# Splitting the input of a gated feed-forward stage before its norm factor is known, and applying the factor where the products are read

## The reference, cut to what matters

```python
def rms_norm(x, g):                 # per token: x * rsqrt(mean(x*x) + eps) * g
def conv_glu_ffn(h, w_up, conv_w, w_down):      # first block, width 2816 twice
    up = causal_dwconv(h @ w_up, conv_w)        # 3 taps over tokens, per channel
    gate, val = jnp.split(up, 2, axis=-1)
    return (jax.nn.silu(gate) * val) @ w_down
def sq_relu_mlp(x, w_up, w_down):               # second model's blocks, width 4096
    h = jax.nn.relu(x @ w_up); return (h * h) @ w_down
# first block: x = x + mixer(norm(x)); x = x + conv_glu_ffn(norm(x)); x = norm(x)
# then twice:  h = h + concat(mixer, memory_attention)(norm(h)) @ w_out
#              h = h + sq_relu_mlp(norm(h))
```

## Time and profile before

| what | us |
|---|---|
| timed, median of 3 runs (lowest, highest) | 1092.79 (1085.38, 1100.64) |
| the profiled execution's own time | 1086.28 |
| its span, first to last instruction | 1084.5 |
| busy: PE, DVE, ACT, POOL | 1036.2, 681.2, 548.7, 91.5 |
| granted TensorE clock, mean | 0.993 |

### The profile page before, as it was taken

One profiled execution on the slowest core, in us unless ns is written; L12 is line 12 of the kernel. 1 busy time (PEld: TensorE's weight loads), 2 busy tenths in 40 slices (PEclk: granted clock), 3 DMA queues, 4 the chain that ended last, 5 costly groups with the idle time before them and its releaser, 6 DMA issues.

```text
span 1084.5 us, 20595 instructions
## 1 busy us (share of the span) xinstructions
PE 1036.2 (96%) x8615; PEld 993.9 (92%) x8615; DVE 681.2 (63%) x807; ACT 548.7 (51%) x714; POOL 91.5 (8%) x54
## 2 busy tenths in 40 slices
PE   4998999899999899999999999999999999999998
PEld 3988779899887799999989899999999989999998
DVE  4777365655375778778677575555566867655553
ACT  4554435443454565555556454444456765544442
POOL 0050021200010000000019510000000001000000
PEclk9999899999999999999999999999999999999999
DMA  6544232324261364554524355555554323655551
GB/s 251 195 157 155 78 117 85 111 79 156 78 221 74 121 231 160 204 216 163 180 87 144 129 190 194 199 182 205 182 176 147 118 79 120 219 205 178 209 178 55
DMA packets 24803, 168.77 MB, mean 156 GB/s; under 512 B 2753, under 2 KB 3137, under 8 KB 5154
## 3 DMA queue, kind: packets, MB, share of 16 engines
q1 hardware_dynamic: 23616, 164.64, 43.2%
q10 hardware_dynamic: 1122, 3.19, 0.9%
HBM read 166.76 MB, written 1.05 MB: 155 GB/s over the span
## 4 chain that ended last, share of the span: by engine, by line
PE 71%; DVE 14%; ACT 7%; POOL 4%; issue 3%; DMA 1%; SPq 0%; ACTq 0%; DVEq 0%
PE G L577 11%; PE G L578 11%; PE G L579 11%; PE D L577 8%; PE D L578 8%; PE D L579 8%; DVE wlo L1704 4%; ACT whi L1199 2%; PE M L578 2%; PE M L577 2%; PE M L579 2%; PE D L821 1%; POOL zp L551 1%; ACT ss L1655 1%; DVE cv L2072 1%
## 5 line engine op out<-in xcount | busy, mean ns | idle before, releaser
L1704 DVE TENSOR_TENSOR wlo<-raw,whi 128x2048 fp32r<-128x2048 f32 (+1 forms) x156 | 360.3, 2314 | 142.6 <-ACT whi L1199 142.5
L577 PE MATMUL G<-xh,whi 128*128 128x256 f32 (+1 forms) x1360 | 387.5, 285 | 12.2 <-DVE wlo L1704 6.6
L578 PE MATMUL G<-xl,whi 128*128 128x256 f32 (+1 forms) x1360 | 379.4, 279 | 0.0
L579 PE MATMUL G<-xh,wlo 128*128 128x256 f32 (+1 forms) x1360 | 379.2, 279 | 0.0
L1199 ACT ACTIVATE whi<-raw 128x2048 fp32r<-128x2048 f32 (+1 forms) x156 | 295.5, 1897 | 54.1 <-PE D L579 50.9
L577 PEld LDWEIGHTS G<-xh,whi 128*128 128x128 f32 (+1 forms) x1360 | 256.6, 189 | 21.8 <-DVE wlo L1704 9.7
L578 PEld LDWEIGHTS G<-xl,whi 128*128 128x128 f32 (+1 forms) x1360 | 256.7, 189 | 1.3 <-issue 1.2
L579 PEld LDWEIGHTS G<-xh,wlo 128*128 128x128 f32 (+1 forms) x1360 | 256.3, 188 | 0.0
L577 PE MATMUL D<-hh,whi 128*128 128x256 f32 x688 | 190.2, 276 | 3.0 <-DVE wlo L1704 1.9
L579 PE MATMUL D<-hh,wlo 128*128 128x256 f32 x688 | 190.0, 276 | 0.0
L578 PE MATMUL D<-hl,whi 128*128 128x256 f32 x688 | 190.0, 276 | 0.0
(11 more groups left out here) (377 smaller groups left out, 1350.3 us busy)
## 6 DMA issues: line engine op xcount, KB each, us to landing
raw<-wall_dram SPq DMA_DIRECT2D x152, 1024.0 KB, 4.8
raw<-wnarrow_dram SPq DMA_DIRECT2D x4, 768.0 KB, 4.4
x<-x_dram SPq DMA_DIRECT2D x4, 256.0 KB, 5.7
mem<-mem_dram ACTq DMA_DIRECT2D x1, 1024.0 KB, 5.2
out_dram<-x SPq DMA_DIRECT2D x4, 256.0 KB, 2.5
poolw<-pool_w_dram ACTq DMA_DIRECT2D x1, 576.0 KB, 7.0
cst<-cst_dram ACTq DMA_DIRECT2D x1, 416.0 KB, 8.9
lora<-lora_dram ACTq DMA_DIRECT2D x1, 256.0 KB, 6.7
```

The lines of the kernel that those rows point to most:

```text
L577: mm(out, w_h, hi, start=start, stop=False, skip_group_check=skip)
L578: mm(out, w_h, lo, start=False, stop=False, skip_group_check=skip)
L579: return mm(out, w_l, hi, start=False, stop=stop, skip_group_check=skip)
L1704: signal(tt(wlo[:, pan.slot, 0:w], raw[:, pan.slot, 0:w], f32(whi[:, pan.slot, 0:w]), SUB), "w_lo")
```

## The change

The gated stage now works as the squared-ReLU stages do. Each part of x is split into `mh`, `ml` (times the gain alone) as soon as its `wo` panel has been added; the squares are summed by POOL and then by four matmuls behind the first up panel; the factor is multiplied in by DVE when it reads an up panel's product into `upad`. ACT's copy from PSUM goes away, and its tap instructions now read `upad`. DVE's gating moves from right after the taps to behind the next panel split. The memory rows are scaled and split in the last groups of `ffn 0` (and for the second block, of `ffn 1`), now into `xh`, `xl`. All other norm inputs use `mh`, `ml`. Both strings of constant matmuls around `ffn 0` are gone.

```diff
-    W += [("mem_load",), ("panel", PAN["wo"]), ("panel", PAN["wo"] + 1), ("mem_squares",)]
-    W += [("panel", PAN["wo"] + 2), ("mem_stat",), ("panel", PAN["wo"] + 3)]
-    W += [("norm", 1), ("mem_scale", 0), ("mem_norm", 0), ("ffn", 0), ("squares", 2)]
+    W += [("mem_load",), ("panel", PAN["wo"]), ("part", 1, 0), ("panel", PAN["wo"] + 1), ("mem_squares",), ("part", 1, 1)]
+    W += [("panel", PAN["wo"] + 2), ("mem_stat",), ("part", 1, 2), ("panel", PAN["wo"] + 3), ("part", 1, 3)]
+    W += [("sums", 1), ("ffn", 0), ("squares", 2)]
...
+    LATE = [(NI1 - 4, NI1 - 3), (NI2 - 3, NI2 - 2)]
+    IN_B = ("in0q", "in0m", "in1", "in1b", "ffn", "ffn0", "ffn1")
```

On PE:

```diff
-            elif n == 1:
-                warm(19, "D0")
...
-                    if nu == 2 and js == 1 and u == 0:
-                        warm(11, "M1")
...
-                    if isinstance(j, int) and j == 0 and f:
-                        norm_stat(2 * f + 2)
+                    if isinstance(j, int) and j == 0 and u == 0:
+                        norm_stat(FNORM[f])
```

On ACT, in `up`:

```diff
-                        fn(upad[:, u, :, 2:T + 2], G[u][:, :, :], ACT.Copy)
+                        act.wait_ge(S(f"up_read{f}"), 2 * j + u + 1)
                         for s_ in range(2):
-                            ins = fn(cv[:, u, s_, :], G[u][:, s_, :], ACT.Copy, scale=w2)
-                        signal(ins, f"up_read{f}")
+                            signal(fn(cv[:, u, s_, :], upad[:, u, s_, 2:T + 2], ACT.Copy, scale=w2), "tap")
```

On DVE, in `up`, and what it calls:

```diff
+                        if u:
+                            gate(j, 0, js)
+                        dve.wait_ge(S("pe_panel"), pan.p + 1)
+                        signal(tt(upad[:, u, :, 2:T + 2], G[u][:, :, :], rstd[:].unsqueeze(1).broadcast_to([P, 2, T]), MUL),
+                               f"up_read{f}")
...
+            def gate(j, u, js):
+                t = 2 * j + u
+                dve.wait_ge(S("silu_e"), t + 1)
+                Step(t, 2, 1)(stt(sgm[:, u, :], sgm[:, u, :], 1.0, cv[:, u, 0, :], ADD, MUL))
+                signal(stt(hid[:, js % 3, u, :], sgm[:, u, :], 0.5, cv[:, u, 1, :], MUL, MUL), "prod")
...
+            def late(i):
+                if i == LATE[f][0]:
+                    mem_scale(f)
+                if i == LATE[f][1]:
+                    for h in range(2):
+                        dve.wait_ge(S("mem_h"), 2 * f + h + 1)
+                        ins = tt(xl[:, 4 * h:4 * h + 4, :], mwk[:, 4 * h:4 * h + 4, :], f32(xh[:, 4 * h:4 * h + 4, :]), SUB)
+                    signal(ins, "mem_l")
```

More of the change, by code:

```diff
@@ L160, in build @@
     rtmp = place("rtmp", [P, T])
-    arena = h_end["wlo"] + 36 * K - 96
+    arena = h_end["wlo"] + 36 * K - 64
     top[0] = arena
@@ L457, in ffn_walk @@
             pair(i, 0, 0)
+            if late is not None:
+                late(i)
         down(ni - 1, Pan(p0 + ni * (nu + 1) - 1), ni - 1, True)
@@ L1261, in parts @@
                 for k in (2 * i, 2 * i + 1):
-                    ins = fn(xh[:, k, :], x[:, k, :], ACT.Copy, scale=pcol(gain, g0 + k))
+                    ins = fn(mh[:, k, :], x[:, k, :], ACT.Copy, scale=pcol(gain, g0 + k))
                 signal(ins, "xh")
@@ L1286, in ahead @@
             split_to(p + 3)
[L1288 to L1293, removed]
         def parts5b():
@@ L1519, in up @@
                         signal(fn(hh[:, js % 3, :, :], rel[:, js % 3, :, :], ACT.Square), f"hid_h{f}")
-                if nu == 2 and js == 0:
-                    high_hid(0, 1, 0)
             def down(i, pan, js, last):
-                tail = isinstance(i, int) and i == ni - 2
-                if not tail:
-                    more(pan, 2)
-                if nu == 2 and not last:
-                    high_hid(i + 1, 1, js + 1)
-                if tail:
-                    more(pan, 2)
+                if nu == 2 and isinstance(i, int) and i == ni - 2:
+                    high_hid(ni - 1, 1, js + 1)
+                more(pan, 2)
+            def late(i):
+                if i == LATE[f][1]:
+                    act.wait_ge(S("mem_n"), f + 1)
+                    act.wait_ge(S("pe_panel"), PAN[("wo", "wout0")[f]] + 4)
+                    for h in range(2):
+                        signal(fn(xh[:, 4 * h:4 * h + 4, :], mwk[:, 4 * h:4 * h + 4, :], ACT.Copy), "mem_h")
             def more(pan, ahead):
@@ L1751, in norm @@
             a, b, _, (gain, g0) = NORMS[n]
-            w = wk if n == 0 else wk2
             for i in range(4):
-                scaled(w, x, rstd, gain, i, "nrm", g0)
-                if n == 0 and i == 0:
+                scaled(wk, x, rstd, gain, i, "nrm", g0)
+                if i == 0:
                     split_to(1)
-                low(b + i + 1, i, w[:, 2 * i:2 * i + 2, :])
-            if n == 1:
-                dve.wait_ge(S("pe_panel"), PAN["out3"] + 1)
-                signal(nc.vector.memset(upad[:, :, :, 0:2], 0.0), "zeros2")
+                low(b + i + 1, i, wk[:, 2 * i:2 * i + 2, :])
         def final_norm():
```

133 lines of the change are left out of this document (68 added, 65 removed).

## The result

| | before | after |
|---|---|---|
| time, median of 4 runs (us) | 1095.38 (1085.38 to 1100.64) | 1132.12 (1130.77 to 1133.59) |
| ratio, 95% interval | | 1.0347, 1.0268 to 1.0426 |
| profiled execution: own time, span | 1086.28, 1084.5 | 1131.53, 1129.7 |

The forecast was 1116 (1099 to 1130). First the head of the page of the changed kernel, the same lines as the earlier trace rows, and the line of its part 4 that gives the shares of the chain that ended last.

The account below looks back on a forecast made before the run. PE was taken to bound the kernel before; after the change the ring of ACT and DVE would bind the gated loop. ffn 0 would end at 563.3 instead of 532.95: +30.3, less 0.5, span 1114.3, forecast 1116 us (1099 to 1130).

Parts of the forecast that it names:

- 0.9 us to spare in the loop: Gated loop before the change: PE needs 16.32 us per group, the ring of ACT and DVE 15.38.
- The ring: Gated loop: ACT and DVE wait on each other's split and taps; 19.8 us per group after, PE idle 3.5.
- ACT's first tap: Gated loop: ACT's first tap and the handoff to DVE enter each half between read and taps, 0.57 us.
- the short ring: Rival, gated loop: handoffs and taps cheaper, 19.1 down to 18.0 us per group, 1098 to 1111; chance 0.22.
- the unbound ring: Rival, gated loop: additions at most 0.94 us per group, PE stays the bound, 1068; chance 0.07.
- The memory rows: Groups 8 and 9 of the gated stage: scaling and splitting them on DVE adds 5.6 us to the path.
- The first panel's other three quarters cover 4.1 us, so PE waits 1.0: Entry: PE works on x's ready pairs while the last is prepared, ending the first up panel at 338.8.
- The clock swallowed by idle time: Gated loop: a lower PE clock decides only below 0.82; above that, PE's idle time absorbs it.
- The chance given to the clock: Rival, gated loop: mean clock 0.75, PE needs 21.8 us per group, 1134 in all; chance 0.07.
- "Nothing" for `ffn 1` and `ffn 2`: ffn 1: the second block's memory rows find room on DVE and cost nothing, bound 3 us.
- the 6.5 us to the median that I noted as 0.6%: Base: the profiled execution, 1086.28, stood 0.6% under the median 1092.79 of three runs.

Follow-up runs that it names:

- e1: Changed kernel with the loop's old order put back and the factor left out of the gated stage; 1092.63 us, 1.0064 times the kernel before.
- e7: Changed kernel with ACT's next panel split moved ahead of the tanh, right behind the taps; 1092.62 us, 1.0004 times the kernel before.
- e5: Changed kernel with DVE's gating of a half moved ahead of the next panel split; 1114.01 us, 1.0192 times the kernel before.
- e6: Changed kernel with PE's wait for D0 to D3 moved ahead of the first down panel; 1128.86 us, 1.0335 times the kernel before.
- e11: Changed kernel with the edits of e7, e6 and e9 together; 1083.13 us over 12 runs, 0.9913 times the kernel before.
- e10: Changed kernel with 11 constant matmuls ahead of the second up panel of every group but the first; 1130.68 us, 1.0339 times the kernel before.
- e2: Kernel before with only its arena starting 32 bytes higher, as in the changed kernel; 1097.17 us, 1.0115 times the kernel before.
- e3: Changed kernel with the arena put back 32 bytes lower, where it was before; 1126.89 us, 1.0385 times the kernel before.
- e13: Kernel before, unchanged, executed and profiled again; 1091.12 us.
- e12: Kernel before, unchanged, executed and profiled again; 1088.28 us.
- e8: Changed kernel with 96 bytes left free behind upad; 1128.90 us, 1.0321 times the kernel before.
- e9: Changed kernel with 992 bytes left free behind upad; 1126.76 us, 1.0288 times the kernel before.
- e14: Kernel before, unchanged, executed and profiled again; 1092.61 us.

## Why the prediction was wrong, point by point

- **PE bounds the kernel before, with 0.9 us to spare in the loop**: right. e1 and e7 both return to PE's pitch.
- **The ring, 19.8 us per group, 3.5 of them idle on PE**: right, 19.98. The gating was priced at 0.82 and gave 0.79 (e5). Waits for ACT's first tap were 0.54 and 0.80, priced 0.57. PE's idle time per group was 2.7 rather than 3.5, and at times 1.6, since its panels had become longer. Of the rivals, the short ring and the unbound ring did not come.
- **The memory rows, 5.6 us on the path in the gated stage**: 3.25 + 2.36 on DVE at 520.73 and 543.14, as priced. From factor to last down panel I had 214.7 us, the trace has 213.0 (348.43 to 561.46).
- **"The first panel's other three quarters cover 4.1 us, so PE waits 1.0"**: this step failed. The wait for `D0` to `D3` at the top of `ffn`, in the code of both kernels, was not read. Before, the statistic and the constant matmuls stood in front of it and hid it; the change took that cover away. PE waited 3.00 and ran part of the panel at half rate, and the factor was 5.2 us late, 3.6 of which belong to it (1.6 came from upstream). e6 and e11 show the entry as I had drawn it: from the start of the last `wo` panel to the first read 16.5 us in both, predicted 16.9 (343.2 less 326.35), 20.5 in the changed kernel.
- **The clock swallowed by idle time**: right in the loop (e10), wrong at the end. The last down panel starts behind a wait of 6.77 us and its matmuls stand 160.6 ns apart: 7.71 us for the predicted 5.4, and nothing hides it. The chance given to the clock spoke of a mean over the loop, not of the single panels behind a wait. The constant matmuls of e10 do not help there (169.4 ns), since none of them stands ahead of that panel.
- **"Nothing" for `ffn 1` and `ffn 2`**: this step failed by 9.0 us. I had costed the moved work and not the moved addresses, though the first line of the diff is an address. e2 shows that 32 bytes cost this in the kernel before. Putting them back in the changed kernel (e3) returned only 5.2 us, since its up panels now read `mh` and not `xh`, at 117.3 ns there. So the term is the place of all moved operands; by what mechanism it acts stays open.

Sum over the profiled executions: predicted 30.3 less 0.5, measured 45.2; the difference of 15.4 is 1.6 upstream, 3.6 entry, 1.7 less in the ring, 2.3 last panel, 9.0 + 0.5 behind it (the parts are rounded). The upstream part is inside the scatter of these profiles (324.57 to 328.69 for the same start). The entry, the last panel and the addresses are costs of the change; without the addresses alone the time would be near 1123 by this sum.

**The base** was a lucky one too. The profiled execution before (1086.28) has 113.3 ns in all three feed-forward stages, and of the 6.5 us to the median that I noted as 0.6% one stage at the other pitch would explain 5.1 (e13 against e12). The changed kernel has no such good executions: its addresses gave 118.2 (down) and 113.6 to 114.2 (up) in `ffn 1` and `ffn 2` of every profile taken with them (after, e1, e2, e5, e6, e7, e10). Against 1085 its addresses cost 12 us, against the median of 1093 about 4. I left that distance out of the sum as noise; it was a cost with a cause.

## What to carry to other kernels

When two engines hand a weight split to each other, write their ring out by their orders in the program and count every instruction that the change puts inside it: that gave the loop within 1%, and it also names the repair, which is to move the split ahead of the instruction that waits (e7). When a change takes work away in front of a wait, read every wait that this work had hidden, those for free banks included. And when a change moves buffers, compare the pitch of the same matmuls in stages that the change does not touch, before any wait is explained.

## What the runs showed of the hardware

- How fast 128x256 matmuls follow one another at clock 1.00 changes when buffers are moved by as little as 32 bytes (e2: down panels 113.3 to 118.2 ns, up panels 113.3 to 114.0). By the byte of the moving operand `hh`, a down panel ran at 113.3, 113.5 or 117.7 ns with 182336, 113.3 or 117.7 with 183360, 118.2 with 182368, 119.6 with 182400, 117.7 with 182464. `mh` at 127040 gave 113.5 to 114.2 or 117.8, at 127008 117.3. The three bytes at which 113.3 to 114 was seen in these two buffers (182336, 183360, 127040) lie 64 above a multiple of 1024, the others do not. But that it is the operand's own byte which counts is not shown: other buffers moved with it in every run, and panels whose operand had not moved changed too (`xh` in e2, `mh` in e8 and e9). It is an observation, and its cause is open.
- The same program on the same addresses settles, where PE has no waits, for a whole stage at 113.3 or at 117.7 ns (e12 against e13 and e14; e11's `ffn 1` against its `ffn 2`). A gated stage at 117.7 takes 5.1 us more. This makes a good part of the scatter between 1085 and 1093. Where PE waits, the pitch changes within a stage: in the changed kernel's gated stage up panels on the same `mh` follow at 120.0 ns (from 451.90) and at 114.0 (from 473.30).
- Panels that PE starts behind a wait can run partly at the lower clock level, 148.7 ns (at 336.98) and 160.6 (at 561.46) on average over 48 matmuls, with granted clocks of 0.76 and 0.72 over the panel. Here waits of about 2.7 us once per group gave it only in some groups: the up panel at 440.59 ran at 115.6 ns and clock 1.00, the one at 460.58, behind the same wait, at 146.7 and 0.80. The Trainium skill's "TensorE: Matmul & The Clock Gate", section "HAM oscillation — how this bites in real kernels", says that a PE that waits once per tile can fall to the half rate at each and pay for it each time; this trace agrees only in part.
